# A hybrid attention and mixture-of-experts kernel: the pair's down product in front of the dense down product's second tile, latents and softmax steps at other places, layers written out

## The reference: what is computed

```python
for layer in range(DEPTH):                       # DEPTH = 2
    parts = jnp.split(x @ w_in[layer], IN_SPLITS, axis=-1)
    mixed = jnp.concatenate([_fox_group(...),    # 4 heads, decay from the forget logits f
                             _dsa_group(...),    # the index scores keep 64 of up to 256 keys
                             _mla_group(...),    # queries and keys from normed latents c_q, c_kv
                             _chunk_band_group(...)], axis=-1)
    x = _layer_norm(ALPHA * x + mixed @ w_out[layer], ln1_g[layer], ln1_b[layer])
    ffn = _moe(x, ...)                           # 64 experts, 8 per token, and a shared expert
    x = _layer_norm(ALPHA * x + ffn, ln2_g[layer], ln2_b[layer])

def add_expert(e, acc):                          # for each of the 64 experts
    h = xt @ w_gu[e]
    a = jax.nn.silu(h[:, :D_EXPERT]) * h[:, D_EXPERT:]
    return acc + (a * gates_t[e][:, None]) @ w_down[e]
```

## Time and profile before

| | |
|---|---|
| median of 3 runs | 1805.72 us (1804.13 to 1807.51) |
| the profiled execution | 1801.29 us, of it 1799.5 us span |
| granted TensorE clock, mean | 0.973 of full |
| PE busy | 1664.7 us (93%) |
| DVE, ACT, POOL busy | 952.0, 765.8, 283.5 us |
| chain that ended last | PE 64%, DMA 15%, DVE 7%, issue 5%, ACT 5% |
| HBM read and written | 507.24 and 21.77 MB, 294 GB/s over the span |

### The profile page before, as it was taken

How to read it: one execution, slowest core, us unless ns; L and a number is a source line. 1 busy time by engine, 2 the same in 40 slices (tenths; PEclk the granted TensorE clock), 3 DMA queues, 4 the chain that set the end, 5 groups by cost and what they waited for, 6 DMA issues and landing times.

```text
span 1799.5 us, 29297 instructions
## 1 busy us (share of the span) xinstructions
PE 1664.7 (93%) x10062; PEld 1260.4 (70%) x10062; DVE 952.0 (53%) x1445; ACT 765.8 (43%) x1020; POOL 283.5 (16%) x200
## 2 busy tenths in 40 slices
PE   6798899999999999999879989999999999999996
PEld 5697767766776677666668877666776667777763
DVE  1746455555555555555457455555555555555555
ACT  3464434343434443444246633444444444434342
POOL 6471000001000001000135700000010000000010
PEclk8899899999999999999989989999999999999998
DMA  9331599999999999999953327999999999999993
GB/s 312 95 118 59 208 335 350 345 346 350 341 350 353 356 352 352 353 341 336 338 182 115 118 71 287 345 349 342 356 355 351 346 351 354 354 341 349 347 356 113
DMA packets 141739, 529.71 MB, mean 294 GB/s; under 512 B 12236, under 2 KB 51576, under 8 KB 108408
## 3 DMA queue, kind: packets, MB, share of 16 engines
q1 hardware_dynamic: 122288, 467.77, 69.1%
q0 software_dynamic: 15440, 56.11, 11.2%
q10 hardware_dynamic: 3960, 5.17, 0.9%
HBM read 507.24 MB, written 21.77 MB: 294 GB/s over the span
## 4 chain that ended last, share of the span: by engine, by line
PE 64%; DMA 15%; DVE 7%; issue 5%; ACT 5%; DVEq 2%; SPq 1%; ACTq 0%; PEldq 0%
DMA raw<-in_w_exp_gu_dram 11%; PE ps L1083 11%; PE ps L1057 10%; PE ps L949 7%; PE ps L950 7%; PE ps L951 7%; PE ps L733 6%; PE ps L986 4%; PE ps L972 4%; ACT w_hi L1405 3%; DMA raw<-in_w_exp_down_dram 3%; DVE o_lo L1791 2%; PE ps L1124 2%; PE ps L979 2%; PE ps L865 1%
## 5 line engine op out<-in xcount | busy, mean ns | idle before, releaser
L1763 DVE TENSOR_TENSOR raw_r<-raw,w_hi 128x2048 fp32r<-128x2048 f32 x192 | 440.0, 2293 | 447.6 <-ACT w_hi L1405 447.5
L1405 ACT CAST w_hi<-raw 128x2048 fp32r<-128x2048 f32 x192 | 365.8, 1906 | 311.2 <-DMA raw<-in_w_exp_down_dram 203.9
L949 PE MATMUL ps<-x_hi,w_hi 128*128 128x256 f32 x1088 | 311.4, 286 | 1.8 <-DVE x_lo L1689 1.8
L950 PE MATMUL ps<-x_lo,w_hi 128*128 128x256 f32 x1088 | 306.9, 282 | 0.0
L951 PE MATMUL ps<-x_hi,raw_r 128*128 128x256 f32 x1088 | 306.3, 282 | 0.0
L1083 PE MATMUL ps<-raw,xc 128*64 128x512 f32 x1024 | 233.8, 598 | 0.0
L949 PEld LDWEIGHTS ps<-x_hi,w_hi 128*128 128x128 f32 x1088 | 206.6, 190 | 31.4 <-issue 30.1
L950 PEld LDWEIGHTS ps<-x_lo,w_hi 128*128 128x128 f32 x1088 | 207.9, 191 | 1.5
L951 PEld LDWEIGHTS ps<-x_hi,raw_r 128*128 128x128 f32 x1088 | 206.7, 190 | 0.0
L682 POOL DMA_INDIRECT xg_b<-x_by_token,token_b x32 | 31.3, 979 | 830.9 <-DVE token_c L1742 830.9
L1083 PEld LDWEIGHTS ps<-raw,xc 128*64 128x64 f32 x1024 | 67.8, 136 | 119.4 <-issue 115.0
(11 more groups left out here) (324 smaller groups left out, 2916.6 us busy)
## 6 DMA issues: line engine op xcount, KB each, us to landing
raw<-in_w_exp_gu_dram SPq DMA_DIRECT2D x256, 1024.0 KB, 8.0
raw<-in_w_exp_down_dram SPq DMA_DIRECT2D x128, 1024.0 KB, 7.7
raw<-in_w_in_dram SPq DMA_DIRECT2D x22, 1024.0 KB, 5.8
raw<-in_w_out_dram SPq DMA_DIRECT2D x8, 1024.0 KB, 5.2
row_b<-gates_by_rank SPq DMA_DIRECT2D x30, 256.0 KB, 5.8
row_c<-gates_by_rank SPq DMA_DIRECT2D x60, 128.0 KB, 5.3
raw<-in_w_sh_gu_dram SPq DMA_DIRECT2D x4, 1024.0 KB, 5.1
row_a<-gates_by_rank SPq DMA_DIRECT2D x32, 128.0 KB, 10.8
```

The source lines that it names most:

```text
L949: nc.tensor.matmul(o, h, x_hi[:, c, :], start=(first and i == 0), stop=False, skip_group_check=True)
L950: nc.tensor.matmul(o, h, x_lo[:, c, :], start=False, stop=False, skip_group_check=True)
L1405: nc.scalar.copy(w_hi[CAST[j] % 3][:], raw[:, j % RING, 0:UNIT_F]).then_inc(hi_done, 1)
L1763: nc.vector.tensor_tensor(raw_r[:, s, 0:UNIT_F], raw[:, s, 0:UNIT_F], w_hi[CAST[j] % 3][:], ALU.subtract)\
```

## The change

In every pass but the last, PE does the dense down product AD of tile 0, then C1D and C2D, then AD of tile 1 (before: both tiles of AD, then C1D and C2D). SP takes the slots in the order in which they come free (`LAST_USES`): C20, A1, C10. In the last pass of a layer the pair's down product comes first, then B's scatter, AD of tile 0 and its scatter, and AD of tile 1 and its scatter by halves; `layer_norm` takes a tile's halves as they come (`ready`).

In the attention part the index key comes out of unit 1's row job (ACT repeats its 32 columns, PE transposes them) and the forget logits out of unit 3's, made 260 wide (`tile_rows`); the two narrow jobs are gone, and there are 13 jobs. All units after 3 are projected one place earlier against the rest of PE's list: unit 4 in front of the wait for the latents. DVE does the latents' variance before the index scores and the norm right after them; the bias tables and all rounds of `mark_top` come later, the rounds between the softmax steps. ACT and DVE split the shared expert's first unit earlier, and POOL subtracts its second one (`shared_lo1_done`). The shared gate product's first part, and the first projection of a layer, do all matmuls on x_hi first and those on x_lo last. The four matmuls on zeros that open PSUM for the sums stand just in front of the wait for `a_ready`; ACT does the shared silu earlier. POOL clears the DRAM sums after its splits, not before. The layers are written out twice on each engine.

The diff, cut to its core:

```diff
-    LAST_JOB = [0, 2, 3, 5, 6, 7, 8, 9, 10, 11, 12, 13]
+    LAST_JOB = [0, 1, 2, 4, 5, 6, 7, 8, 9, 10, 11, 12]
...
+    LAST_USES = (0, 1, 2, 4, 5, 3)
...
+    USED = [B0, B1, A0, C10, C20, A1, C11, C21, BD, C1D, C2D, AD]
...
-                    for j in range(RING):
+                    for j in LAST_USES:
...
-            with pool.Fori(0, DEPTH) as layer:
-                for t in range(NT):
-                    pool.dma_start(added_rows[t * P:(t + 1) * P, :].rearrange("p (c n) -> p c n", n=P),
-                                   zeros[:].bitcast(F32).unsqueeze(1).to_broadcast([P, KC, P])).then_inc(sums_cleared, 16)
+            for layer in range(DEPTH):
...
+                    pool.dma_start(added_rows[t * P:(t + 1) * P, :].rearrange("p (c n) -> p c n", n=P),
+                                   zeros[:].bitcast(F32).unsqueeze(1).to_broadcast([P, KC, P])).then_inc(sums_cleared, 16)
+                pool.wait_ge(hi_done, done(layer, hi_done, 2))
+                pool.tensor_tensor(raw_r[:, slot(NPRE + 1), 0:UNIT_F], raw[:, slot(NPRE + 1), 0:UNIT_F], w_hi[1][:], ALU.subtract)\
+                    .then_inc(shared_lo1_done, 1)
...
+                if k == 0 and first:
+                    wh, wl = high_part(k), in_slot(k, width(k), raw_r)
+                    for c in range(KC):
+                        if c % 4 == 0:
+                            pe.wait_ge(w_lo_ready, done(layer, w_lo_ready, c // 4 + 1))
+                        pe.wait_ge(xt_hi_sb, done(layer, xt_hi_sb, c // 2 + 1))
+                        nc.tensor.matmul(o, wh[:, c, c0:c0 + n], x_hi[:, c, :], start=(c == 0), stop=False)
+                        nc.tensor.matmul(o, wl[:, c, c0:c0 + n], x_hi[:, c, :], start=False, stop=False)
+                    for c in range(KC):
+                        pe.wait_ge(xt_sb, done(layer, xt_sb, c // 2 + 1))
+                        last = nc.tensor.matmul(o, wh[:, c, c0:c0 + n], x_lo[:, c, :], start=False, stop=(c == KC - 1))
+                    return last
...
                 transpose_x(layer, 0, x_next, 1 - NT, xt_ps)
                 project_t(0, 0)
-                columns(job(1)[0:IDM, 0:SEQ], layer, 1, 0, IDM, True).then_inc(job_ps, 1)
-                project_rows(2, 1)
-                pe.wait_ge(job_sb, done(layer, job_sb, 2))
+                project_rows(1, 1)
+                o = job(2)
+                rows(o, layer, 2, (0,))
+                pe.wait_ge(ik_rows_sb, done(layer, ik_rows_sb, 1))
+                for t in range(NT):
+                    last = nc.tensor.transpose(ps[:, 4, t * P:(t + 1) * P], ik_rows[:, t].rearrange("p r n -> p (r n)"), ident[:])
+                last.then_inc(ik_ps, 1)
+                rows(o, layer, 2, (1,)).then_inc(job_ps, 1)
+                pe.wait_ge(ik_sb, done(layer, ik_sb, 1))
                 index_dots(1)
-                project_rows(3, 2)
-                project_rows(4, 3)
-                columns(job(5)[0:NH, 0:SEQ], layer, 3, GW, NH, False).then_inc(job_ps, 1)
+                tile_rows(job(3), layer, 3, 0).then_inc(job_ps, 1)
+                tile_rows(job(4), layer, 3, 1).then_inc(job_ps, 1)
+
+                project_t(5, 4)
                 pe.wait_ge(index_read, done(layer, index_read, 1))
                 index_dots(0)
-
                 pe.wait_ge(latent_ready, done(layer, latent_ready, 1))
...
+                pe.wait_ge(job_sb, done(layer, job_sb, 5))
+                for t in range(NT):
+                    last = nc.tensor.transpose(ps[0:NH, 5, SEQ + t * P:SEQ + (t + 1) * P], f_tok[:, t, :], ident[:])
...
-
+
+                project_t(6, 5)
...
+                pe.wait_ge(f_read, done(layer, f_read, 1))
...
-                project_t(7, 5)
...
+                project_t(7, 6)
...
+                project_rows(9, 8)
...
+                pe.wait_ge(job_sb, done(layer, job_sb, 9))
+                query_key("band", 0)
+                project_t(10, 9)
...
+                        if f == FC - 1 and u == 1:
+                            last.then_inc(shared_gate_ps, 1)
...
+                o = ps[:, 0, 0:SEQ]
+                for u in range(2):
+                    hi, lo = hi_slot(u, u), piece_slot(slot(NPRE + u), u, raw_r)
+                    s, n = ((split_done, done(layer, split_done, 1)), (shared_lo1_done, layer + 1))[u]
+                    pe.wait_ge(s, n)
+                    for i in range(4):
+                        c = 4 * u + i
+                        pe.wait_ge(x_hi_sb, done(layer, x_hi_sb, c // 2 + 1))
+                        nc.tensor.matmul(o, hi[:, i, 0:P], x_hi[:, c, :], start=(c == 0), stop=False, skip_group_check=True)
+                        nc.tensor.matmul(o, lo[:, i, 0:P], x_hi[:, c, :], start=False, stop=False, skip_group_check=True)
+                for c in range(KC):
+                    pe.wait_ge(xt2_sb, done(layer, xt2_sb, c // 2 + 1))
+                    nc.tensor.matmul(o, hi_slot(c // 4, c // 4)[:, c % 4, 0:P], x_lo[:, c, :], start=False, stop=(c == KC - 1),
+                                     skip_group_check=True)
...
-                for b in range(2 * NT):
-                    nc.tensor.matmul(ps[:, 4 + b, :], zeros[:], x_hi[:, 0:2, :], start=True, stop=False, skip_group_check=True)
...
+                for b in range(2 * NT):
+                    nc.tensor.matmul(ps[:, 4 + b, :], zeros[:], x_hi[:, 0:2, :], start=True, stop=False, skip_group_check=True)
...
-                    for t in range(NT):
-                        last = dense_down(t, *weights(AD))
-                    last.then_inc(unit_used, 1)
-
-                    if final:
-                        pe.wait_ge(place_b_ready, done(layer, place_b_ready, it + 1))
-                        pe.wait_ge(b_out_sb, done(layer, b_out_sb, 2))
-                        for t in range(NT):
-                            scatter(place_b, t)
+                    if not final:
+                        dense_down(0, *weights(AD))
...
+                    if final:
+                        pe.wait_ge(place_b_ready, done(layer, place_b_ready, it + 1))
+                        pe.wait_ge(b_out_sb, done(layer, b_out_sb, 2))
+                        for t in range(NT):
+                            last = scatter(place_b, t)
+                        last.then_inc(b_added, 1)
+                        dense_down(0, *weights(AD))
+                        pe.wait_ge(place_c_ready, done(layer, place_c_ready, it + 1))
+                        pe.wait_ge(c_out_sb, done(layer, c_out_sb, it * 2 + 2))
+                        scatter(place_c, 0).then_inc(tile0_done, 1)
+                        for half in range(2):
+                            last = dense_down(1, *weights(AD), (half,))
+                            if half == 1:
+                                last.then_inc(unit_used, 1)
+                            scatter(place_c, 1, (half,)).then_inc(moe_done, 1)
+                    else:
+                        dense_down(1, *weights(AD)).then_inc(unit_used, 1)
...
+                relus(1)
...
+                for t in range(NT):
+                    o = bank(3 + t)
+                    if t == NT - 1:
+                        split_pre(5)
+                    nc.scalar.copy(v_tok["fox"][:, t, :], o[:, 0:GW])
+                    nc.scalar.copy(f_tok[:, t, :], o[:, GW:GW + NH]).then_inc(job_sb, 1)
+                bank(5)
+                split_pre(6)
+                column_job(5, qk_t["fox"][0][:], HD ** -0.5)
+                relus(0)
...
+                split_pre(NIN)
...
+                shared_hi(0)
                 probs_out("dsa", 1)
+                shared_hi(1)
...
+                act.wait_ge(shared_gate_ps, done(layer, shared_gate_ps, 1))
+                silu_dense(0)
...
+                    if final:
+                        act.wait_ge(b_added, done(layer, b_added, 1))
...
-                nc.vector.scalar_tensor_tensor(xt, xt, scale, ps[:, bank:bank + 2, :].rearrange("p a n -> p (a n)"),
-                                               ALU.mult, ALU.add)
-                dve.drain()
-                for half in range(2):
-                    nc.vector.bn_stats(stats[:, t, half, :], x_tok[:, t, half * 512:(half + 1) * 512])
+                for half, (s, n) in enumerate(ready):
+                    part = x_tok[:, t, half * 512:(half + 1) * 512]
+                    dve.wait_ge(s, n)
+                    nc.vector.scalar_tensor_tensor(part, part, scale, ps[:, bank + half, :], ALU.mult, ALU.add)
+                    dve.drain()
+                    nc.vector.bn_stats(stats[:, t, half, :], part)
...
-                dve.wait_ge(params_loaded, (layer + 1) * 16 * PARAMS)
...
-                index_scores(1)
-                mark_top(1, 4)
                 dve.wait_ge(sums_ready, done(layer, sums_ready, 1))
...
-                mark_top(1, 2)
+                index_scores(1)
...
+                dve.wait_ge(params_loaded, (layer + 1) * 16 * PARAMS)
+
+                for bias, by_distance in ((band_bias, hankel), (t5_bias, t5_hankel)):
...
```

(24 more changed lines are left out.)

209 lines of the change are left out of this document (87 added, 122 removed).

## The result

The changed kernel takes 1756.28 us (median of 4 runs, 1754.22 to 1760.68), the kernel before on the same chip 1806.62: ratio 0.9714, 95% interval 0.9672 to 0.9756. Five later runs gave 1751.19 and a ratio of 0.9699 (0.9661 to 0.9737). The forecast was 1761. The profiled execution has a span of 1753.6 us, 45.9 less than before.

What follows compares the result with a forecast made beforehand. PE, busy 1664.7 of 1799.5 us, was taken as the bound, so only vanished matmuls and gaps count. Terms summed to -44.2 us, 1801.3 to 1757.1, forecast as a 1761 us median; own range 1750 to 1772, 8 in 10 1742 to 1780.

Steps and rivals of the forecast that it cites:

- The loop, 0: Expert loop, 30 passes: 0 us, since o_lo still waits for B1's low part; bounds -42 to +45 us.
- Attention to the fox scores, -10.3 and +0.3: First projection to fox scores: first layer -10.3 us as the latents' wait goes, second +0.3 for four more transposes.
- Fox scores on, -4.4 and -3.5: Fox scores through the next four jobs: one unit fewer saves 5.9 us; new mla-copy wait charged 1.5 and 2.4.
- First layer norm, router, -9.5 a layer: Mla scores to first expert product: layer norm -5.3 us, clock -1.2, router and shared expert -3.0, each per layer.
- the layer norm's 5.3: First layer norm, each layer: PE's 8.78 us idle falls to 3.5 through earlier, halved work: -5.3 us.
- End of a layer, -3.2, -3.3, -0.8: Last pass: earlier norm of tile 0, -3.2 and -3.3 us; next layer's first projection on x_hi before x_lo, -0.8.
- The clock: First layer norm: a shorter stop leaves less following work at the low clock, -1.2 us each, between 0 and 3.4.
- The other outcome that I gave: First layer norm: transposes do not count as activity for the clock gate, so the clock's term would be 0.
- Rival 2: Attention's gains eaten: POOL's splits hold DVE, mla copies 4 us late, low clock: +12 to +20, 1773 to 1781; chance 0.12.

Runs made afterwards that it cites:

- the part alone: Kernel before with only the pair's down product between AD's two tiles and slots refilled as they come free, except in a layer's last pass: 1806.56 us, ratio 1.0006.
- the second profile: Changed kernel run once more without any edit: 1751.19 us, ratio 0.9699.
- The router's part alone: Changed kernel with the four matmuls on zeros and the shared silu back in their old places: 1759.51 us, ratio 0.9751.
- the run above: Changed kernel with four mark_top rounds on tile 1 behind the fox group's biased_max instead of in front of it: 1753.68 us, ratio 0.9708.

## Why the prediction was right, by its own steps

- **The loop, 0.** Right, and for the reason given: the part alone gives 1.0006, and the chain is unchanged. (The two profiles of the changed kernel have 38.1 and 35.0 us on o_lo, of the forecast's 40.) What was missed is what it makes possible: moving o_lo ahead of B1's low part gains 17 us with the new order and loses 54 with the old one.
- **Attention to the fox scores, -10.3 and +0.3.** Measured -8.4 and -0.9. The latents' stop went. The first layer fell short at its start: I had allowed 1.4 us for the low clock there, but the matmuls run at the low level (one every 0.21 us in place of 0.12) for the first 8.6 us of the projection, 6.7 in the second profile, where the kernel before had 3; and PE idles 1.5 us in the stretch. So part of what the earlier start gains is lost again to the clock. That the second layer would not care for DVE's order was half wrong: it moved little because two things cancel. The index key now comes out of unit 1's row job through ACT and a transpose, its dot products start 22.3 us behind the first projection (16.5 before), and DVE's index scores come 2.8 us later than before in the first layer and 4.0 in the second, counted from the projection. With the rounds still ahead of the norm, both layers lose 9 us, the second too. The order of DVE pays for the removed jobs.
- **Fox scores on, -4.4 and -3.5.** Measured -4.8 and -3.2; the new stop is where it was forecast, on mk_t, at 3.6 and 2.5 us (I had charged 1.5 and 2.4).
- **First layer norm, router, -9.5 a layer.** Measured -10.2 and -8.5. PE idles 3.8 us in the last of the five windows above; 3.5 was worked out. That stretch alone went from 17.50 to 10.40 us, 7.1 less, where -5.3 and -1.2 were forecast. The router's part alone is worth some 3 us a layer by the traces, as forecast. Of the layer norm's 5.3, POOL's subtraction accounts for 1.2 by the stops on x_tok.
- **End of a layer, -3.2, -3.3, -0.8.** Measured -4.8 and -2.8, but the terms behind it were different: the order of the last pass gives 2.1 in the first layer by the stretch (2.4 to 2.8 by the stop on x_tok), and writing the layers out, which I charged at nothing, gives 3.3 at the border.
- **Not seen:** -4.4 us at the start, from POOL's clearing transfers. It stood in the change and I gave it no term. The wait on POOL's raw_r is the third longest of the kernel before, ahead of the latents' 9.4 us, and I had not taken it up in the earlier trace rows:

```profile
PE ps L733 <- POOL raw_r L666: 11.1, 2, 10.6
```

  With the 3.3 us of the point before, the measured -45.9 us hold 7.7 us that the forecast of -44.2 did not know. They were made up for by pass 0 (+2.4 and +1.4), 1.9 us less at the first layer's attention, 1.9 less from the last pass's order at the border (2.1 of 4.0) and 1.0 less in the second layer behind the mla scores. That the sums meet within 2 us is in part luck.
- **The clock.** From the end of the output projection to the router's first product the first layer has 7.1 us less: 5.0 of idle time (8.78 to 3.79) and 2.1 of PE's busy time (8.72 to 6.61) for the same work (42 and 43 matmuls), which I read as the clock: 0.63 over 17.5 us, 13 us at the low level, against 0.84 over 10.4 us, 3.3 us. I had taken 1.2, between 0 and 3.4. The other outcome that I gave, no gain at all because of the transposes in the stop, did not come; what part the transposes have no row separates, since the stop became shorter too. With the shared activation's 2.6 us this makes 9.7 of the 10.2 us between the mla scores and the experts. In the second layer the same stretch gives 7.2 us, and something else between the mla scores and the experts costs some 1.3.
- **Rival 2** named DVE held by POOL. It is there in places: the normalization of 128x1024 took 2.43 us in the run above against 1.23 in the changed kernel, with POOL's subtraction beside it from 88.69 on. The Trainium skill, "SBUF — State Buffer", section "Who interferes with whom", has this for operations with both inputs in SBUF; the trace agrees. But POOL's new subtraction lies beside additions that read PSUM, at 0.68 and 0.67 us per 128x512, as fast as without it, and giving it back to DVE did not gain: 1.2 us of stop more a layer, 2 to 5 us by the ratios, which is not clear of the noise. Where both inputs are in SBUF the changed kernel pays too: the band group's normalization of 128x1024 took 3.17 us beside 5.69 us of POOL's split. What this costs in all no run shows.
- **Pass 0, +2.4 and +1.4** in the first profile, -1.3 and +0.9 in the second: no term, and none needed.

## What to carry to other kernels

A reordering that moves nothing by itself can be what makes the next edit pay: look at what stands between the product that now ends early and the one who waits for it, and move that too, but only with the new order in place. When a wait has gone, read which engine has the most work between the two points where it was; moving the same work behind instead of ahead moved the stop to the next link and left the time. Give a term to each thing in the change, the transfers that a queue issues first and the loops written out among them: two that had none were worth 4.4 and 3.3 us in the traces. And list every long wait before choosing: the one that the clearing transfers moved was the third longest.
